# A table of gates built by scatter-adds from GpSimd instead of matmuls of one-hots

## What is computed

```python
s1 = jnp.einsum('bshd,hnd->bshn', q[..., 0, :], sub_k1)
s2 = jnp.einsum('bshd,hnd->bshn', q[..., 1, :], sub_k2)
v1, i1 = lax.top_k(s1, PEER_TOPK)
v2, i2 = lax.top_k(s2, PEER_TOPK)
cand = (v1[..., :, None] + v2[..., None, :]).reshape(B, S, PEER_HEADS, PEER_TOPK * PEER_TOPK)
vs, ci = lax.top_k(cand, PEER_TOPK)
eidx = e1 * PEER_NKEYS + e2
gates = jax.nn.softmax(vs, axis=-1)
act = jax.nn.gelu(jnp.einsum('tkd,td->tk', expert_u[ib], xb))
return jnp.einsum('tk,tkd->td', act * gb, expert_v[ib])
```

## Time and profile before

| | us |
|---|---|
| median of 3 runs | 3006.87 (3006.38 to 3007.98) |
| the profiled execution, its own time | 3007.15 |
| its span, first to last instruction | 3005.4 |
| expert stage, first half (TensorE) | 1466.2 to 2261.3 |
| expert stage, second half and last gate | 2261.5 to the end |
| L2203, 448 records of 275 ns each, overlapping | 54.8 busy |

### The profile page before, as it was taken

The page is one execution under the profiler, slowest core; times in us unless marked ns, Lnnn a source line. Parts: engine busy times, 40 slices in busy tenths (PEclk is TensorE's granted clock), DMA queues, the critical chain, the costliest instruction groups (busy, mean ns, idle before and its releaser), DMA issues.

```text
span 3005.4 us, 42961 instructions
## 1 busy us (share of the span) xinstructions
PE 2962.8 (99%) x17085; PEld 2678.9 (89%) x17085; DVE 2020.9 (67%) x2869; ACT 1488.6 (50%) x2274; POOL 169.0 (6%) x312
## 2 busy tenths in 40 slices
PE   8999999999999999999999999999999999999999
PEld 7998778888888888978789999999999999999999
DVE  5656654444445445554557988888888888888876
ACT  4355544444444444454444466447745555555553
POOL 2000000000000002140000000000010000000000
PEclk9999999999999999999999999999999999999999
DMA  7554355556554554535667779778999899899764
GB/s 255 160 169 154 114 169 193 189 188 193 184 195 182 194 189 150 169 109 208 190 208 249 237 261 338 238 222 293 337 371 360 300 328 321 310 322 318 264 221 141
DMA packets 238382, 690.73 MB, mean 230 GB/s; under 512 B 14249, under 2 KB 95177, under 8 KB 203392
## 3 DMA queue, kind: packets, MB, share of 16 engines
q1 hardware_dynamic: 221024, 598.71, 59.2%
q0 software_dynamic: 12608, 71.73, 6.3%
q10 hardware_dynamic: 4576, 17.89, 1.6%
HBM read 652.61 MB, written 33.57 MB: 228 GB/s over the span
## 4 chain that ended last, share of the span: by engine, by line
PE 51%; DVE 0%; ACTq 0%; ACT 0%; issue 0%; DVEq 0%
PE banks L2156 16%; PE banks L2232 14%; PE banks L2157 8%; PE banks L2233 7%; PE banks L2203 2%; PE banks L2253 1%; PE banks L2255 1%; PE banks L2254 1%; PE banks L2175 0%; DVE peer_features L378 0%; DVE weights_lo L195 0%; PE banks L2192 0%; PE banks L2221 0%; ACTq L2310 0%; DVE residual L2585 0%; DVE peer_scratch L2584 0%
## 5 line engine op out<-in xcount | busy, mean ns | idle before, releaser
L195 DVE TENSOR_TENSOR weights_lo<-weights,weights_hi 128x1024 fp32r<-128x1024 f32 (+4 forms) x1080 | 1228.5, 1179 | 701.8 <-ACT weights_hi L188 700.0
L188 ACT ACTIVATE weights_hi<-weights 128x1024 fp32r<-128x1024 f32 (+4 forms) x1080 | 1046.4, 1017 | 1316.8 <-PE banks L419 640.8
L2156 PE MATMUL banks<-peer_features,weights_hi 128*128 128x448 f32 (+1 forms) x2304 | 738.9, 377 | 2.7 <-DVE weights_lo L195 2.7
L417 PE MATMUL banks<-weights_hi,features_hi 128*128 128x512 f32 (+3 forms) x1600 | 605.2, 378 | 12.5 <-DVE weights_lo L195 9.3
L2157 PE MATMUL banks<-peer_features,weights_lo 128*128 128x224 f32 (+1 forms) x2304 | 615.3, 267 | 0.0
L419 PE MATMUL banks<-weights_hi,features_lo 128*128 128x512 f32 (+3 forms) x1600 | 600.5, 375 | 0.0
L418 PE MATMUL banks<-weights_lo,features_hi 128*128 128x512 f32 (+3 forms) x1600 | 600.4, 375 | 0.0
L2232 PE MATMUL banks<-peer_features,weights_hi 128*128 128x448 f32 x1568 | 492.4, 374 | 0.0
L2156 PEld LDWEIGHTS banks<-peer_features,weights_hi 128*128 128x128 f32 x2304 | 432.0, 187 | 44.2 <-DVE weights_lo L195 3.2
L2157 PEld LDWEIGHTS banks<-peer_features,weights_lo 128*128 128x128 f32 x2304 | 438.6, 190 | 0.0
L2233 PE MATMUL banks<-peer_features,weights_lo 128*128 128x224 f32 x1568 | 414.3, 264 | 0.0
(11 more groups left out here) (406 smaller groups left out, 2757.7 us busy)
## 6 DMA issues: line engine op xcount, KB each, us to landing
weights<-in_expert_u SPq DMA_DIRECT2D x128, 1024.0 KB, 5.5
weights<-in_expert_v SPq DMA_DIRECT2D x128, 1024.0 KB, 7.2
weights<-in_w_ffn_gate SPq DMA_DIRECT2D x44, 1024.0 KB, 5.1
weights<-in_w_ffn_up SPq DMA_DIRECT2D x44, 1024.0 KB, 5.1
weights<-in_w_ffn_down SPq DMA_DIRECT2D x44, 1024.0 KB, 4.8
weights<-in_w_in SPq DMA_DIRECT2D x48, 900.0 KB, 4.7
weights<-in_w_out SPq DMA_DIRECT2D x32, 1024.0 KB, 5.1
weights<-in_w_in SPq DMA_DIRECT2D x24, 704.0 KB, 4.2
```

Of the source, the lines that this page charges most:

```text
L188: act.activation(hi[:, k, n], raw[:, k, n], ACT.Copy).then_inc(self.hi_ready, 1 + skip)
L195: last = dve.tensor_tensor(lo[:, k, n], raw[:, k, n], hi[:, k, n].bitcast(F32), ALU.subtract)
L417: pe.matmul(out, xh, wh, start=first, stop=False)
L2156: pe.matmul(self.bank(n % 3, 2 * (T - lo)), wh[:, k, :], F[:, k, :, lo:T], start=(k == 0), stop=False)
```

## The change

1. The table of gates is no longer made by matmuls. VectorE computes for each choice the number of its cell in DRAM (second key x 128 x 224 + first key x 224 + token), and GpSimd adds the gate to that cell by an indirect DMA with an add: one DMA for each slot of the 128 choices and each token tile, 256 in all, of 128 (or, in the tile with the gathered tokens, 96) values of 4 bytes. Within a head the 16 cells of a token differ, so the 16 DMAs of a head run freely; before the next head GpSimd waits until all have landed. `one_hots`, `hot_act`, the transposes of the choice, the matmuls of L2203, the copies out of PSUM and the 14 stores of the table are gone.
2. The table must be zero before. GpSimd stores 16 blocks of zeros of 0.9 MB in the feed-forward, one in each half of rounds 1 to 8. The table's layout is now `[second key][first key][token]`, so that a reload reads 7 KB in one piece for each partition, not 14 pieces of 512 bytes.
3. The gathered tokens are the last 32, not the first 32, and their tile is chosen first, from step 10; the other tile from step 44 (before: 22 and 74). The scores are made four steps before each part is chosen, not in steps 18 to 25. Each part is signalled when its gates are ready (`chosen`, eight parts, not two tiles). Rows are summed from step 79 on, in five steps of six up to 125, then in each.
4. GpSimd's program: 160 scatters with the first three gathers behind the first three, then a gather and four scatters in turn up to gather 26, then the other gathers.
5. SyncE's first reload of the table waits for all 256 scatters.

The diff, cut to its core (the other changed lines only move the dense tokens from columns 32 to 255 to columns 0 to 223, or name the new tiles and semaphores):

```diff
-    WQ = 384
+    WQ, ROWS, ZEROED = 384, 32, 8
...
+                        self.pool_chain.on(pool)(pool.memset(zeros[:, :], 0.0))
+                        parts = NKEYS // self.ZEROED
+                        for n in range(parts):
+                            pool.wait_ge(ring.used, ring.done(1 + n // 2, 4 * (n % 2)))
+                            pool.dma_start(self.g_d[:, self.ZEROED * n:self.ZEROED * (n + 1), :],
+                                           zeros[:, :].rearrange("p (e t) -> p e t", e=self.ZEROED)).then_inc(self.gates_zeroed, 16)
+                        pool.wait_ge(self.gates_zeroed, 16 * parts)
...
-        SC, RET, TURN = 18, (22, 74), (55, 107)
-        ROWS, BUFS = 32, 3
-        HOT = [(58 + i, 0, ROWS // 8 + i) for i in range(16 - ROWS // 8)] + [(110 + i, 1, i) for i in range(16)]
-        SUM = [56, 57, *range(58, 74), *range(108, 142), *range(V0 - 1, V0 + 8), *range(V0 + 9, V0 + 12)]
+        FIRST, RET = NT - 1, (44, 10)
+        ROWS, BUFS = self.ROWS, 3
+        SUM = [s for s in range(78, 126) if s % 6] + [*range(126, 142), *range(V0 - 1, V0 + 7)]
         DOTS = SUM[-1] + 1
         free = [s for s in range(V0 + 17, V0 + 118) if (s - V0) % 16 not in (0, 5, 6, 8, 10, 14)]
         ADD = [free[k * len(free) // (2 * ROWS)] for k in range(2 * ROWS)]
+        order_of = lambda t: (t - FIRST) % NT
+        SCORE = [RET[(FIRST + q // 4) % NT] + 8 * (q % 4) - 4 for q in range(4 * NT)]
...
-        g_d = nc.dram_tensor("expert_gates", (P, BLKS, NKEYS, BLK), F32, kind="Internal").ap()
+        g_rows, g_d, zeroed = self.g_rows, self.g_d, self.gates_zeroed
...
-            gblk = scratch[:, 0:4096].rearrange("p (b e t) -> p b e t", b=2, t=BLK)
-            hot = [x.rearrange("p (g w c e) -> p g w c e", g=2, w=2, c=4) for x in (XN[:, 0, :], scratch[:, 4096:6144])]
             s_in = [XN[:, 1 - b, 0:8 * DENSE].rearrange("p (e t) -> p e t", t=DENSE) for b in range(2)]
-            g_in = [scratch[:, b * 2048:b * 2048 + 8 * DENSE].rearrange("p (b e t) -> p b e t", b=BLKS, t=BLK) for b in range(2)]
+            g_in = [scratch[:, b * 2048:b * 2048 + 8 * DENSE].rearrange("p (e t) -> p e t", t=DENSE) for b in range(2)]
...
-            egT = eg[:, 3:6, :]
+            gates_of, cell_of = eg[:, 2:4, :], eg[:, 4:6, :].bitcast(U32)
+            token, token_i = tmp("token_number", [P, NT]), tmp("token_number_i", [P, NT], I32)
...
+                    dve.sem_inc(chosen, 1)
...
+                    ch(dve.tensor_scalar(vif[:, 0:2, :].rearrange("p h k -> p (h k)"), eg[:, 0, slots], float(DENSE), token[:, t:t + 1],
+                                         ALU.mult, ALU.add))
+                    ch(dve.scalar_tensor_tensor(out=cell_of[:, t, slots], in0=eg[:, 1, slots], scalar=float(NKEYS * DENSE),
+                                                in1=vif[:, 0:2, :].rearrange("p h k -> p (h k)"), op0=ALU.mult, op1=ALU.add))
+                    if t == FIRST:
...
-                            sp.wait_ge(chosen, NT)
+                            sp.wait_ge(chosen, NT * PARTS)
...
                             else:
-                                for b in range(2):
-                                    sp.wait_ge(gates_out[b], 8 * BLKS)
-                                sp.wait_ge(gated, DENSE // 4)
-                            sp.dma_start(g_in[g % 2], g_d[:, :, 8 * g:8 * g + 8, :]).then_inc(g_back[g % 2], 16)
+                                sp.wait_ge(scattered, 16 * NT * SLOTS)
+                            sp.dma_start(g_in[g % 2], g_d[:, 8 * g:8 * g + 8, :]).then_inc(g_back[g % 2], 16)
...
+                    def gather(c):
...
+                    def scatter(n):
+                        t, slot = (FIRST + n // SLOTS) % NT, n % SLOTS
+                        tokens = P - ROWS if t == FIRST else P
+                        if slot % TOPK == 0:
+                            pool.wait_ge(chosen, n // (HP * TOPK) + 1)
+                            if slot > 0:
+                                pool.wait_ge(scattered, 16 * n)
+                        pool.indirect_dma_start(out=g_rows[:, :], in_=gates_of[0:tokens, t, slot:slot + 1], in_offset=None,
+                                                compute_op=ALU.add,
+                                                out_offset=bass.IndirectOffsetOnAxis(ap=cell_of[0:tokens, t, slot:slot + 1], axis=0))\
+                            .then_inc(scattered, 16)
+
+                    pool.wait_ge(zeroed, 16 * NKEYS // self.ZEROED)
+                    early, mixed = SLOTS + HP * TOPK, 4
+                    for n in range(early):
+                        scatter(n)
+                        if n < BUFS:
+                            gather(n)
+                    for c in range(BUFS, 2 * ROWS):
+                        gather(c)
+                        for n in range(early + mixed * (c - BUFS), min(early + mixed * (c - BUFS + 1), NT * SLOTS)):
+                            scatter(n)
...
-                        if 0 <= n - SC < NT * PARTS:
-                            q = n - SC
-                            t, part = q // PARTS, q % PARTS
+                        if n in SCORE:
+                            q = SCORE.index(n)
+                            t, part = (FIRST + q // PARTS) % NT, q % PARTS
...
-                                pe.wait_ge(tile_read, U0)
+                            pe.wait_ge(tile_read, U0 if q >= PARTS else 4 * part + 4)
...
-                        if n in TURN:
-                            if n > BACK[-1]:
-                                pe.wait_ge(*x_back(KD // 2))
-                            pe.wait_ge(chosen, TURN.index(n) + 1)
-                            for c in range(3):
-                                last = pe.transpose(self.bank(5, P, c * P), eg[:, c, :], self.ident[:, :])
-                            last.then_inc(choice_turned, 1)
...
-                        for t, r, place_in_order in hot_step(n):
-                            for g in (2 * r, 2 * r + 1):
-                                gi = 2 * place_in_order + g % 2
-                                pe.wait_ge(hots, gi + 1)
-                                pe.wait_ge(hots_act, gi + 1)
-                                if gi >= 2:
-                                    pe.wait_ge(gates_read, gi - 1)
-                                h = hot[g % 4 // 2][:, g % 2]
-                                for c in range(4):
-                                    last = pe.matmul(self.bank(3 + g % 2, P, c * P), h[:, 0, c, :], h[:, 1, c, :],
-                                                     start=True, stop=True)
-                                last.then_inc(gated, 1)
-                    pe.wait_ge(gates_read, DENSE // 4)
-                    pe.wait_ge(choice_read, NT)
+                    pe.wait_ge(spread_read, 1)
...
-                        for t, r, place_in_order in hot_step(s - 2):
-                            blk, nth = t * 8 + r // 2 - ROWS // BLK, place_in_order // 2
-                            for g in (2 * r, 2 * r + 1):
-                                act.wait_ge(gated, 2 * place_in_order + g % 2 + 1)
-                                if g % 4 == 0 and nth == 0:
...
-                                act.dma_start(g_d[:, blk], gblk[:, nth % 2]).then_inc(gates_out[nth % 2], 16)
...
-                    def one_hots(g, gi):
-                        if gi >= 4:
-                            dve.wait_ge(gated, gi - 3)
...
-                            s4 = s_in[g % 2][:, e, :].rearrange("p e (b t) -> p e b t", t=BLK)
-                            dve.tensor_tensor(s4, s4, g_in[g % 2][:, :, e, :].rearrange("p b e t -> p e b t"), ALU.mult)\
+                            dve.tensor_tensor(s_in[g % 2][:, e, :], s_in[g % 2][:, e, :], g_in[g % 2][:, e, :], ALU.mult)\
...
+        dense = T - self.ROWS
+        self.g_rows = nc.dram_tensor("expert_gates", (P * NKEYS * dense, 1), F32, kind="Internal").ap()
+        self.g_d = self.g_rows.rearrange("(p e t) o -> p e (t o)", e=NKEYS, t=dense)
+        self.gates_zeroed = self.sem("expert_gates_zeroed")
```

More of the change, by code:

```diff
@@ L2082, in retrieval @@
                             row_gate[quarter * 32:quarter * 32 + 32, 0, :].rearrange("p (c k) -> p c k", k=8),
-                            eg[0:ROWS, 2, :].rearrange("p (c q k) -> p c q k", q=4, k=8)[:, :, quarter]))
-                dve.sem_inc(chosen, 1)
+                            gates_of[P - ROWS:P, NT - 1, :].rearrange("p (c q k) -> p c q k", q=4, k=8)[:, :, quarter]))
                 yield
```

116 lines of the change are left out of this document (35 added, 81 removed).

## The result

The change makes the kernel slower: **3036.27 us** (median of 4 runs, 3035.63 to 3037.36) against 3007.29 us (4 runs, 3006.38 to 3007.98), a ratio of 1.0097, 95% interval 1.0079 to 1.0114. The forecast was 2958 us with a range of 2954 to 3006 us, so the sign was wrong. The profiled execution took 3035.63 us, its span is 3033.9.

A forecast was written before the change was run, and what follows sets the result against it. The prediction took TensorE's own work to bound the kernel: 3007.15 us, less 50.8 us leaving TensorE, plus 1.5 us for the wait at the table reload, gives 2957.9, so 2958 us, range 2954 to 3006 us.

The forecast's parts named there:

- What leaves TensorE: 28 table steps at 1.79 us and two blocks of choice transposes leave TensorE's queue: 50.8 us less.
- Zeros, choosing from step 10: Zero stores in the feed-forward and choosing from step 10 on VectorE: cost taken as 0 each.
- Price of one issue: GpSimd's time per scatter, read from gathers of 128 indices: 1.38 us, within bounds of 1.24 and 2.23 us.
- The gather read as evidence against a hold-up: A gather of 0.96 us at 1632.16 ran full speed inside VectorE's low-part operation, so VectorE was taken not to delay GpSimd.
- The first deadline: Gather 3, behind 160 scatters, reached by GpSimd at 1870 us, issuable from 1887, wanted by 1907.7; limit 1.61 us a scatter.
- The stated point of decision: Ahead of gather 3, the scatter price from which late GpSimd makes the kernel slower than before: 1.95 us.
- rival 1: GpSimd late at 2.23 us a scatter, 101 us past the limit at gather 3: 3071 us, chance 0.10.
- The window's lower end: Gather 3 may go only once the first row is summed, at the end of TensorE's step 79: 1887 us.
- The alternating part: A gather and four scatters per summed row take GpSimd 8.2 us, fitting the row's 12, later 10 us.
- The second deadline: SyncE waits 12 us for the last scatters before the table reload, delaying weight loads: 1.5 us of time.
- Rival 3: Adds slow on the DMA engines from 52 ns a packet; at 70 ns 3040 us, chance 0.06.
- Rival 5: VectorE blocks GpSimd's issuing while reading two tensors: 2.65 us a scatter, 3203 us or more, chance 0.03.

The follow-up runs named there:

- half_scatters: The changed kernel with only the 128 scatter-adds of the tile chosen first, the other tile's 128 left out: 2957.18 us, ratio 0.9834 to the kernel before.
- light_vector: The changed kernel with VectorE making low parts of one eighth of each weight tile and row products over 64 of 1024 columns: 2975.56 us.
- light_vector_rows_first: light_vector with 128 scatter-adds in place of 160 ahead of gather 3, then 5 behind each gather: 2992.92 us.
- rows_first: The changed kernel with 128 scatters in place of 160 ahead of gather 3, and 5 in place of 4 behind each gather: 3045.23 us.

## Why the prediction was wrong

- *What leaves TensorE*, 50.8 us: right. Busy time less 49.0 us and time less 49.9 us in half_scatters; plain_write, where only the add is missing, took 2957.99 us, the forecast's 2957.9.
- *Zeros, choosing from step 10*: right, no cost to about 1 us (half_scatters).
- *Price of one issue*, 1.38 us: **this step failed**. It was taken from gathers, which have the number of indices but not the operation. Measured: 2.04 us a scatter, and 2.03 for the 163 issues ahead of gather 3. Put together from undisturbed rows: 1.24 us for a plain write with its gap (0.94 and 0.30), 0.14 less than I had; 0.54 for the add (mean 1.48 us at 96 and 128 tokens against 0.94; light_vector has 382.6 / 256 = 1.49); 0.26 for VectorE's hold-up (1.74 less 1.48). The bound of 2.23 us held; I set the weight inside the bounds by the likeness of the indices.
- *The gather read as evidence against a hold-up*: the second half of the same failure. It started at 1632.16, 0.02 us after the low-part pair at 1632.14, just the phase that costs nothing. One gather shows one phase; 256 scatters meet them all. The third gather, 1.93 us, which I put down as a bound, started 1.29 us into that pair and was held up as scatters at that phase are, by 0.97 us. It stood in the row beside the one that I relied on.
- *The first deadline*: the mechanism was right to a few us. Gather 3 was wanted by 1907.7; reached at 1972.6, with 4 us of reserve, that is 61 us late on TensorE, and the wait was 57.4. The 65 us are 163 x 0.65 = 106 us by the price and 3.7 by the later start (1608.7 in place of 1605), less the 38 us of margin and 6.6 of landings that were shorter (33.4 in place of 40). The stated point of decision, 1.95 us a scatter, lies just under the measured 2.03 us, so it is **rival 1**, at a smaller size: 3036 in place of 3071 us.
- *The window's lower end*: I gave gather 3 both ends (1887 and 1907.7) and used only the upper one in the rivals; light_vector_rows_first shows what the lower one costs: GpSimd stood for 26 us, and the time was 17 us longer than in light_vector.
- *The alternating part*: it fitted, though the 8.2 us of the sum were too few. Four scatters and a gather took 9.5 to 10.9 us, 12.5 to 17.6 with a landing, 11.2 on average over 22 rows. One row, the one right behind gather 3, was late and cost TensorE 2.5 us; rival 1's 18 us did not come.
- *The second deadline*: foreseen as 12 us of SyncE and 1.5 us of time. With scatters 2 us apart it was 23.5 us of SyncE and 12.9 us of TensorE. In plain_write, with scatters in time, it was 11.5 us of SyncE, so the path was worked out rightly. Cured of the first loss alone, the kernel pays at this one (rows_first).
- *Rival 3, slow adds on the DMA engines*: no. In 1922 to 1940 us, with nothing else moving, 1446 packets had 22.0% of 16 engines, 44 ns each, and 32 ns in 1690 to 1710, where the plain ones have 11; the limit was 52. A scatter of 128 tokens leaves 9 packets on each of the 16 engines, not the 8 that I took, which lowers the limit to 46.
- *Rival 5, VectorE keeps GpSimd from issuing*: right in kind, far too large in size: 0.26 us a scatter, not 1.27. A scatter waits for one operation, the one in which it starts, and not for all of the low parts' time.

## What to carry to other kernels

When a change multiplies one kind of instruction, price that kind, with its operation, from a row that has it; where none exists, a likeness (the same number of indices) is no reason to stand at the low end of the bounds, and if the point of decision lies inside them the chances must say so. On an engine that works in its own order, an instruction that waits has a window with two ends: reached too early, it holds back what stands behind it, and that costs as well. One row beside another engine's work shows one phase; ask what the other phases cost before you call the work harmless. And a sum over the whole queue, here 256 issues, 14 landings and the gathers against the time from the first chosen part to the reload, tells before any order is tried whether one can fit.

## What the runs showed of the hardware that I had not expected

- An indirect write of 4-byte values with an add occupies GpSimd for 1.41 us at 64 and 96 tokens and 1.55 at 128, against 0.91 (96) and 0.97 (128) without the add. It leaves one packet a token and 16 more (80, 112, 144), the plain write 32 on average.
- An indirect DMA's issue is held up by a VectorE operation on two SBUF tensors in which it starts, by what is left of that operation less 0.1 us, up to 1.06 us; by nothing if the operation starts after it, or reads one tensor.
- Small scatters land fast: the wait behind a run of 16 is 3.9 us on average, though each of them adds to 96 or 128 places in DRAM.
